# Stick-breaking attention of one hybrid block: attention times V turned round, with a copy and a transpose behind it

## The reference, cut to what matters

```
def stick_breaking(q, k, v):                    # (1, 1024, 8 heads, 64)
    for blk in range(8):                        # 128 queries each
        t0, t1 = 128 * blk, 128 * (blk + 1)
        z = einsum('bthd,bshd->bhts', q[:, t0:t1], k[:, :t1]) * 64 ** -0.5
        ...
        a = where(valid, exp(log_sigmoid(z) + log_stick), 0.0)
        outs.append(einsum('bhts,bshd->bthd', a, v[:, :t1]))
```

## Time and profile before

| | |
|---|---|
| median of 3 runs | 2024.59 us (2021.89 to 2024.75) |
| the profiled execution, own time | 2024.59 us |
| its span | 2022.8 us |
| TensorE busy (matmul) | 1842.6 us, 91% of the span |
| VectorE busy | 807.2 us, 40% |
| ScalarE busy | 426.7 us, 21% |
| GpSimd busy | 653.7 us, 32% |
| mean granted TensorE clock | 0.958 |

### The profile page before, as it was taken

How to read it: one execution, slowest core, us unless ns; L and a number is a source line. 1 busy time by engine, 2 the same in 40 slices (tenths; PEclk the granted TensorE clock), 3 DMA queues, 4 the chain that set the end, 5 groups by cost and what they waited for, 6 DMA issues and landing times.

```text
span 2022.8 us, 25337 instructions
## 1 busy us (share of the span) xinstructions
PE 1842.6 (91%) x9816; PEld 1552.7 (77%) x9816; DVE 807.2 (40%) x1192; ACT 426.7 (21%) x763; POOL 653.7 (32%) x294
## 2 busy tenths in 40 slices
PE   1799799979999998999799897599999999999997
PEld 1687678768898887888688797478888888888886
DVE  6574938470043626263211317561212122221215
ACT  2333424330001111111100223231120202112022
POOL 4010212043342313131334466233344433334440
PEclk8799998989999998999899998799999999999999
DMA  7030221031131101010311153231111111111122
GB/s 305 11 104 1 94 74 63 21 103 44 42 128 43 35 32 35 32 45 21 123 43 41 59 181 107 82 115 42 42 42 61 46 59 41 41 41 41 54 76 99
DMA packets 38082, 135.10 MB, mean 67 GB/s; under 512 B 5864, under 2 KB 6760, under 8 KB 37488
## 3 DMA queue, kind: packets, MB, share of 16 engines
q1 hardware_dynamic: 30320, 109.29, 16.0%
q10 hardware_dynamic: 7680, 24.65, 3.4%
HBM read 121.33 MB, written 12.60 MB: 66 GB/s over the span
## 4 chain that ended last, share of the span: by engine, by line
PE 81%; DVE 10%; issue 5%; POOL 2%; ACT 1%; DMA 0%; DVEq 0%; SPq 0%; ACTq 0%; POOLq 0%
PE ps L370 21%; PE ps L371 21%; PE ps L372 21%; PE ps L429 3%; PE ps L430 3%; PE ps L431 3%; DVE uu L1022 2%; PE ps L472 1%; PE ps L584 1%; DVE sg L975 1%; PE ps L608 1%; PE ps L586 1%; PE ps L585 1%; PE ps L606 1%; PE ps L460 1%
## 5 line engine op out<-in xcount | busy, mean ns | idle before, releaser
L331 POOL TENSOR_TENSOR w_hi<-raw,zero 128x1024 fp32r<-128x1024 f32 x144 | 284.9, 1978 | 1310.1 <-PE ps L372 817.1
L333 POOL TENSOR_TENSOR w_lo<-raw,w_hi 128x1024 fp32r<-128x1024 f32 x144 | 368.8, 2561 | 11.3
L370 PE MATMUL ps<-r_hi,w_hi 128*128 128x512 f32 x640 | 250.6, 391 | 23.6 <-issue 20.8
L372 PE MATMUL ps<-r_hi,w_lo 128*128 128x512 f32 x640 | 252.4, 394 | 0.0
L371 PE MATMUL ps<-r_lo,w_hi 128*128 128x512 f32 x640 | 252.4, 394 | 0.0
L370 PE MATMUL ps<-w_hi,a_hi 128*128 128x256 f32 x768 | 221.8, 289 | 9.9 <-DVE a_lo L1206 5.4
L372 PE MATMUL ps<-w_hi,a_lo 128*128 128x256 f32 x768 | 217.4, 283 | 0.8 <-issue 0.8
L371 PE MATMUL ps<-w_lo,a_hi 128*128 128x256 f32 x768 | 217.8, 284 | 0.0
L370 PE MATMUL ps<-w_hi,f_hi 128*128 128x512 f32 x512 | 202.5, 396 | 0.0
L371 PE MATMUL ps<-w_lo,f_hi 128*128 128x512 f32 x512 | 202.5, 396 | 0.0
L372 PE MATMUL ps<-w_hi,f_lo 128*128 128x512 f32 x512 | 202.5, 395 | 0.0
(11 more groups left out here) (187 smaller groups left out, 3073.6 us busy)
## 6 DMA issues: line engine op xcount, KB each, us to landing
raw<-wstream SPq DMA_DIRECT2D x144, 512.0 KB, 3.3
raw<-ada_rows SPq DMA_DIRECT2D x32, 512.0 KB, 3.3
ada_s<-ada SPq DMA_DIRECT2D x8, 1024.0 KB, 18.5
xs<-x SPq DMA_DIRECT2D x2, 2048.0 KB, 11.3
m_dram<-m1s ACTq DMA_DIRECT2D x1, 4096.0 KB, 12.5
m<-m_dram ACTq DMA_DIRECT2D x1, 4096.0 KB, 13.5
x_dram<-m ACTq DMA_DIRECT2D x8, 512.0 KB, 2.6
out<-m SPq DMA_DIRECT2D x8, 512.0 KB, 2.6
```

The lines of the kernel that those rows point to most:

```text
L331: nc.gpsimd.tensor_tensor(w_hi[:, slot, part], raw[:, h, :], zero[:, 0:1].broadcast_to([P, RAW]), ALU.add).then_inc(w_split, 1)
L333: nc.gpsimd.tensor_tensor(w_lo[:, slot, part], raw[:, h, :], w_hi[:, slot, part].bitcast(f32), ALU.subtract).then_inc(w_split, 1)
L370: nc.tensor.matmul(outp, lh, rh, start=(k == 0), stop=False)
L372: last = nc.tensor.matmul(outp, ll, rh, start=False, stop=(k == chunks - 1))
```

## The change

`times_v` exchanges its operands: the transposed weights (128 keys x 128 queries) are stationary, and the values of one head (64 columns) move. The result comes out as (queries, features) with the two heads side by side in bank 2. `vs` loses its zero columns, and its clearing on GpSimd goes. VectorE copies the result of each block into a new tile `on` at even steps from 4, TensorE transposes that into bank 3 at even steps from 6, and VectorE makes `sbt_hi` and `sbt_lo` from bank 3 at odd steps from 7, now at the beginning of the step, ahead of the scan. TensorE's loop gets two steps more, and VectorE's too. The first `ada_row` of a pair moves into the pipeline (TensorE's step 5 for sub 0 and 11 for sub 1; VectorE's copy one step later), both rows use bank 3, and the second one waits for the last `sbt_lo`. The write of the first row moves forward in SyncE's queue.

```diff
+ADA_ROW = (5, 11)
-                vs = sb("vs", [P, T, 2, 192], f32, c2)
+                vs = sb("vs", [P, T, 256], f32, c2)
+                on = sb("on", [P, P], f32, c2)
...
+                    if n == 7:
+                        row_out(sub, 0)
                     if m == 9:
-                        row_out(0, 0)
                         row_out(0, 1)
...
-                row_out(1, 0)
                 row_out(1, 1)
...
-            nc.gpsimd.memset(vs[:, :, :, :], 0.0).then_inc(vs_zero, 1)
...
                     pe.wait_ge(at_ready, base + u + 1)
-                    if h == 0 and i < 2:
-                        pe.wait_ge(ada_ev, 2 + 2 * G)
-                    elif h == 0:
-                        pe.wait_ge(sbt_ready, 16 * G + 2 * (i - 1))
+                    if h == 0 and i:
+                        pe.wait_ge(on_ready, 8 * G + i)
+                    e = slice((2 * sub + h) * SB_DH, (2 * sub + h + 1) * SB_DH)
                     for b in range(i + 1):
-                        last = nc.tensor.matmul(px[:, 2 + i % 2, 0:P], vs[:, b, sub, h * SB_DH:h * SB_DH + P],
-                                                aT[:, u % 2, b * P:(b + 1) * P],
-                                                start=(h == 0 and b == 0), stop=(h == 1 and b == i))
+                        last = nc.tensor.matmul(px[:, 2, h * SB_DH:(h + 1) * SB_DH], aT[:, u % 2, b * P:(b + 1) * P],
+                                                vs[:, b, e], start=(b == 0), stop=(b == i))
...
                     pe.wait_ge(ada_acc, 8 * G + 4 * (hv + 1))
-                    pe.wait_ge(sbt_ready, 16 * G + 14 + 2 * hv)
-                    nc.tensor.matmul(px[0:1, 2 + hv, :], ones[:, 0:1], acc[:, hv, :], start=True, stop=True).then_inc(ada_mm, 1)
+                    if hv == 0 and sub:
+                        pe.wait_ge(sbt_ready, 16 * G + ADA_ROW[1] - 5)
+                    nc.tensor.matmul(px[0:1, 3, :], ones[:, 0:1], acc[:, hv, :], start=True, stop=True).then_inc(ada_mm, 1)
...
-                for s in range(16 + 3):
+                for s in range(16 + 5):
...
-                ada_row(0)
+                    if s == ADA_ROW[sub]:
+                        ada_row(0)
+                    if s >= 6 and s % 2 == 0:
+                        i = s // 2 - 3
+                        pe.wait_ge(on_ready, 8 * G + i + 1)
+                        if i == (ADA_ROW[sub] - 5) // 2:
+                            pe.wait_ge(ada_ev, 2 + 2 * G + 1)
+                        elif i:
+                            pe.wait_ge(sbt_ready, 16 * G + 2 * i)
+                        nc.tensor.transpose(px[:, 3, 0:P], on[:, :], id_f[:, :]).then_inc(on_tr, 1)
+                pe.wait_ge(sbt_ready, 16 * G + 16)
                 ada_row(1)
...
-                        nc.scalar.activation(vs[:, tok, :, :].rearrange("p a (x d) -> p a x d", x=3)[:, :, 0:3:2, :],
-                                             pg[:, bank, 0:256].rearrange("p (a h d) -> p a h d", a=2, h=2), ACT.Copy).then_inc(ev_act, 1)
+                        nc.scalar.activation(vs[:, tok, :], pg[:, bank, 0:256], ACT.Copy).then_inc(ev_act, 1)
...
-                for s in range(20):
+                for s in range(22):
+                    if s == ADA_ROW[sub] + 1:
+                        ada_row(0)
+                    if s >= 7 and s % 2 == 1:
+                        i = (s - 7) // 2
+                        dve.wait_ge(on_tr, 8 * G + i + 1)
+                        hi, lo = (t[:, ds(G, 1), i * P:(i + 1) * P].rearrange("p a n -> p (a n)") for t in (sbt_hi, sbt_lo))
+                        V.tensor_copy(hi, px[:, 3, 0:P]).then_inc(sbt_ready, 1)
+                        dve.wait_ge(sbt_ready, 16 * G + 2 * i + 1)
+                        V.tensor_tensor(lo, px[:, 3, 0:P], hi.bitcast(f32), ALU.subtract).then_inc(sbt_ready, 1)
                     if s < 16:
...
-                    if s >= 5 and s % 2 == 1:
-                        i = (s - 5) // 2
+                    if s >= 4 and s % 2 == 0 and s <= 18:
+                        i = (s - 4) // 2
                         dve.wait_ge(av_done, 8 * G + i + 1)
-                        hi, lo = (t[:, ds(G, 1), i * P:(i + 1) * P].rearrange("p a n -> p (a n)") for t in (sbt_hi, sbt_lo))
-                        V.tensor_copy(hi, px[:, 2 + i % 2, 0:P]).then_inc(sbt_ready, 1)
-                        dve.wait_ge(sbt_ready, 16 * G + 2 * i + 1)
-                        V.tensor_tensor(lo, px[:, 2 + i % 2, 0:P], hi.bitcast(f32), ALU.subtract).then_inc(sbt_ready, 1)
+                        if i:
+                            dve.wait_ge(on_tr, 8 * G + i)
+                        V.tensor_copy(on[:, :], px[:, 2, 0:P]).then_inc(on_ready, 1)
```

More of the change, by code:

```diff
@@ L222, in build_block @@
         raw_full = [sem("raw_full0"), sem("raw_full1")]
-        zero_set, vs_zero = sem("zero_set"), sem("vs_zero")
+        zero_set = sem("zero_set")
         w_split = sem("w_split")
@@ L236, in build_block @@
         at_tr, at_ready, av_done = sem("at_tr"), sem("at_ready"), sem("av_done")
-        sbt_ready = sem("sbt_ready")
+        on_ready, on_tr, sbt_ready = sem("on_ready"), sem("on_tr"), sem("sbt_ready")
         m1_out, m1_in, cols_in, cols_ready = sem("m1_out"), sem("m1_in"), sem("cols_in"), sem("cols_ready")
@@ L726, in _ @@
             act.wait_ge(n1_split, 32)
-            act.wait_ge(vs_zero, 1)
             with act.Fori(0, STICK_G) as g:
@@ L1014, in ada_row @@
                     dve.wait_ge(ada_mm, 2 + 2 * G + hv + 1)
-                    V.tensor_copy(acc[0:1, hv, :], px[0:1, 2 + hv, :]).then_inc(ada_ev, 1)
-                for s in range(20):
+                    V.tensor_copy(acc[0:1, hv, :], px[0:1, 3, :]).then_inc(ada_ev, 1)
+                for s in range(22):
[8 more added lines that the diff above has]
+                        V.tensor_tensor(lo, px[:, 3, 0:P], hi.bitcast(f32), ALU.subtract).then_inc(sbt_ready, 1)
                     if s < 16:
```

## The result

| | before | changed |
|---|---|---|
| median of 4 runs | 2023.93 us (2021.89 to 2024.75) | 2118.70 us (2115.84 to 2124.49) |
| span of the profiled execution | 2022.8 us | 2110.3 us |
| TensorE busy | 1842.6 us | 1943.0 us |
| mean granted TensorE clock | 0.958 | 0.907 |

The change makes the kernel slower by 95 us: a ratio of 1.0466, interval 1.0442 to 1.0491. The forecast was 2038.5, 14 us slower. The sign is right, the size is wrong by a factor of seven, and the time lies far above the range.

A forecast was written before the change was run, and what follows sets the result against it. TensorE, busy 91% of the span, was taken as the bound, with VectorE setting the pace in pairs (g, 1) from step 6; 3.0 and 3.95 us a pair, twice both, add 13.9 to 2024.59: 2038.5 us, range 2027 to 2047.

The forecast's parts named there:

- What bounds the kernel: Whole kernel: TensorE busy 91% of the span, line 472 only 1.4% of the chain; all other stages keep their lengths.
- I take 0.112 us unchanged, and a gain of nothing: Line 472: loading 128 stationary columns sets the record distance, so 64 moving columns gain nothing over 288 matmuls.
- rival C: New tails of pairs (g, 0): clock falls for 7 us, costing 3.5 us, twice; 2045.6 us; chance 0.16.
- On copies: VectorE's eight copies a pair to `on`: 0.21 us each; 0.4 us exposed in pair (g, 0), 1.05 in (g, 1).
- The row moved forward: First `ada_row`: +0.9 us at step 5 of pair (g, 0), 0.1 at step 6; copy +0.6 and wait 0.6 in (g, 1).
- the wait named in the prediction: Pair (g, 1), step 11: TensorE's row, line 482, waits for VectorE's split of block 2, costing 0.6 us.
- The tails: End of each pair: a strict chain of transposes, copy, splits and row adds 1.7 us; pair (0, 0) 5.55 against 3.84.
- Rival A: Line 472: 64 columns halve its cost, a gain of 14 us; time 2024.6, no change; chance 0.14.
- Rival B: VectorE beside GpSimd's splits: shifted overlaps vanish, over half of 27 us; all gone gives 2011.5; chance 0.08.
- the sum without the row at step 11: Stick-breaking stage: the forecast's total was 13.9 us, 3.0 per pair (g, 0) and 3.95 per pair (g, 1), twice.

The follow-up runs named there:

- the early copy: Changed kernel, 64 columns, with VectorE's copy to `on` at the beginning of its even steps, ahead of scan and product: 2100.48 us, ratio 1.0363.
- the fillers in this kernel: Changed kernel with 128 columns, copy ahead of scan, sub 1's first row at the end, plus unread 256-column matmuls at TensorE's waits: 2061.85 us, ratio 1.0148.
- the kernel before with fillers: Kernel before plus one-pass matmuls of 384 columns that nothing reads, 52 a group, where TensorE waits for VectorE: 2025.03 us, ratio 0.9981.

## Why the prediction was wrong, and what in it was right

**What bounds the kernel.** Right: no stage but this one changed.

**"I take 0.112 us unchanged, and a gain of nothing".** The step that failed. The price is right for all but the second record of each `times_v`, 2.23 us for ten records at half clock and 0.78 for six at full. (The prediction's 0.224 has the last record's end in it; from start to start it is 0.213 at half clock, and 0.112 at full.) What failed is that an unchanged distance means no effect. The earlier trace rows already had the fall of the clock at 141; I priced a fall only for the new tails, in rival C, and took its length, 7 us, for fixed. The runs show that with 64 moving columns a fall at this same place lasts 44 to 51 us (51 in the changed kernel, 48 with the early copy, 44 in the kernel before with 64 columns) and with 128 columns 3 to 14, and what it costs: 47.5 us between the changed kernel and its twin with 128 columns, 45 to 50 between the kernel before and its twin with 64, and 31 us less when work is added. TensorE: Matmul & The Clock Gate of the Trainium skill, section "LDWEIGHTS (loading the stationary operand)", gives 107 ns for the load. The 0.112 us at full clock agree with it, the 0.213 at half clock don't, and neither tells when the clock falls.

**The wait for `on`.** The second step that failed: it isn't there. For each wait that the change adds I should have written who releases it and what stands ahead of that in its queue. `times_v` of block i waits for the copy of block i - 1, which VectorE does behind the product of step 2i + 2, with the weights that `times_v` needs long ready. It is worth 11.5 us with 128 columns and 18 with 64.

**On copies.** 0.21 us each was right where the copy has another instruction behind it: from the copy at 141.50 to the next start at 141.70 there are 0.20.

**The row moved forward.** Pair (0, 0), from scan 5 to scan 7: 9.57 us before, 10.52 after, +0.95, forecast 1.0. At step 11 of pair (0, 1) the wait named in the prediction is there once TensorE is fast enough: 2.29 us ahead of line 482. In the changed kernel TensorE is late anyway and the row runs without a wait, at 255.14. That move was priced at 1.2 us a pair, row copy and wait; with 0.9 a pair back in the tail, undoing it should have taken 2 x (1.2 - 0.9) = 0.6 us off. It took 4.3 by the medians, a difference inside the spread of both kernels: the term may be too small, and these runs don't say by how much.

**The tails.** Right. The end of pair (0, 0) in the changed kernel:

```profile
203.94 0.27 PE L515 MATMUL ps<-id_f,on 128*128 128x128 f32 x1
205.28 0.33 PE L515 MATMUL ps<-id_f,on 128*128 128x128 f32 x1 [1.06 <-DVE sbt_lo L1034]
206.51 1.37 PE L482 MATMUL ps<-acc,ones 128*1 128x512 f32 x2 [0.90 <-DVE sbt_lo L1034]
209.85 0.47 PE L430 MATMUL ps<-qk_hi 64*128 64x128 f32 x1 [1.97 <-DVE qk_lo L1062]
```

5.91 us from the last projection tile to the next pair's scores, forecast 5.55, before 3.84. In pair (0, 1) the tail takes 6.93 us where 5.05 stood, +1.9, forecast +1.7; there its transposes and its row run at half clock, the row's 1.86 us for two records against 1.37.

**Rival A** fell: but for the second record of each `times_v`, which is where the 3.5 us above come from, the distance is the same. **Rival B** fell: VectorE's time moved both ways (line 1006, now 1014, 968 to 877 ns a row; the scan of 640 columns 1482 to 2360, that of 768 2048 to 1758), and over this line, all scans and all products the sum stayed, 204.2 and 204.0 us. **Rival C** held in kind. The stretches of the changed kernel around that tail:

```profile
204.00:208.00 4.00, 1.92 (x5) 0.23 (x3) 1.44 (x6) 0.60 (x1) 0.00 (x0) 0.88 0.00 0
208.00:212.00 4.00, 2.15 (x7) 1.84 (x8) 2.28 (x5) 0.45 (x2) 0.00 (x0) 0.50 0.00 1
212.00:216.00 4.00, 4.00 (x16) 2.90 (x16) 0.58 (x2) 0.45 (x2) 0.00 (x0) 0.76 0.00 0
```

About 7 us at half clock, as forecast for it, with projection tiles behind; the same place before kept 1.00. The tail of pair (1, 0) has the same. What it costs was not measured by itself. It was given 0.16, and where the cover of an engine goes for several us it should have been part of the forecast.

**What stays open.** With the narrow side, the place of the copy and the row at step 11 undone, 25 to 31 us remain. My terms for what is left in that kernel come to 18: the sum without the row at step 11, 13.9 - 2 x 1.2 = 11.5; the row back in two tails, 2 x 0.9; and rival C, 5 at most, since there the clock is at half for 3.4 us behind the tail of pair (0, 0) and for 6.8 behind that of (1, 0). So 7 to 13 us have no term. The lengths show where its loss lies (+11 in the pairs, +12 in the transitions, +6 at the start and the last tail), but not its cause: the fillers in this kernel took 31 us of half clock away and gave no time back, so I can't say how much of it is clock and how much is the longer chain through `on`. A second PSUM bank for the result of `times_v`, which would take its wait away altogether, wasn't tried.

No kernel here with its operands turned round beats the one before. The fastest is the kernel before with fillers, 0.9981 (0.9963 to 0.9999), by less than is worth having.

## What to carry to other kernels

When a change makes matmuls narrower at the same distance, look up every fall of the clock in the trace of before and ask whether what runs behind it will still bring the clock back: in this kernel the answer was worth some 50 us, over three times the 14 that all the copies, transposes and rows were priced at. And for each wait that a change adds, write down the instruction that releases it and what is queued ahead of that one; a buffer that goes from two tiles to one moves its release by a whole step.

## What was not expected of the hardware

- Matmuls whose distance is the same, 0.112 us at full clock with 64, 96 and 128 moving columns (but for the second record of each `times_v`: 0.055, 0.082 and 0.11), differ in what the clock does around them. Two stretches of 10 us, both from 150: granted clock 0.50 with 64 columns, TensorE busy for 10.00; and 1.00 with 128 columns, busy for 8.59. TensorE: Matmul & The Clock Gate of the Trainium skill, section "Part 1: The HAM clock gate", has activity release the throttle. Read as the busy time of the profile, that doesn't fit these two stretches: the clock is low in the one with more of it.
- Work that nothing reads made the kernel faster, 2118.7 to 2087.3 us, and taking work away, in the kernel before with 64 columns, made it slower by 2%.
